# The first two tiles of a stage in one pass over the contraction, and an inverse root in nine dependent steps

## The chip, the cores and the metric

The kernel runs on one core of one Trainium2 chip. Its time is the device time of one execution in microseconds (us). A core has TensorE (PE, with its weight loads shown as PEld), VectorE (DVE), ScalarE (ACT), GpSimd (POOL) and SyncE (SP), which run their own instruction streams and meet at semaphores.

## The reference

A trunk of two layers over 256 tokens of width 1024, all in float32:

```python
for i in range(DEPTH):
    x = x + 0.5 * swiglu(rmsnorm(x, ln_ffn1[i]), w_ffn1_gu[i], w_ffn1_down[i])
    h = rmsnorm(x, ln_mix[i])
    x = x + (even_mixer(h, ...) if i % 2 == 0 else odd_mixer(h, ...))
    x = x + 0.5 * swiglu(rmsnorm(x, ln_ffn2[i]), w_ffn2_gu[i], w_ffn2_down[i])
    gate = jax.nn.sigmoid(rmsnorm(x, ln_ple[i]) @ w_ple_gate[i])
    x = x + gate * (p[i] @ w_ple_proj[i])
return rmsnorm(x, ln_final)

def rmsnorm(x, g):
    return x * lax.rsqrt(jnp.mean(x * x, axis=-1, keepdims=True) + EPS) * g
```

swiglu is (silu(h Wg) * (h Wu)) Wdown with an inner width of 2816. Each mixer is two kinds of eight-head attention between an input and an output projection.

## The kernel before

The residual stream lives transposed in SBUF as xT, [128 features, 8 blocks, 256 tokens]. To keep float32 accuracy in fast matmuls every operand is split into a high and a low part: ACT writes the high part of a weight chunk (L511) and DVE the low part (L746) into wsp, a ring of four chunks of two units each; SP loads the chunks into raw. For the stream, ACT writes the high part of a block (L571, xs_hi) and DVE the low part (L810, xs_lo) into xsA or xsB. A tile is 128 output features by 256 tokens, one PSUM bank; it goes over the KD = 8 blocks of the contraction in tile8. wide_product (L1072, L1073) does a block with two matmuls of 512 and 256 columns, product (L1063 to L1065) with three of 256. `ready` makes a block of the first tile wait for its xs_lo.

There are nine norms, 0 to 8. Norms 0, 2, 4, 6 open a gate/up stage (gate_up), 1 and 5 a mixer's input projection (mixer_in), 3 and 7 the gate of the per-layer embedding (ple, after eight small projection tiles "p"), and 8 the end. A stage starts its matmuls on the stream before it is normalised, and the norm is put in afterwards:

- ACT squares each new block (L574), POOL sums the squares (L465, L468, sq_added).
- column_sums (L1092) adds them over the partitions on PE, into bank 7, one column per 128 tokens. In gate_up and mixer_in it stands behind the first tile, in ple behind tile p4.
- inverse_root on DVE: var (L821), an inverse square root from a shifted bit pattern and three Newton turns (L822 to L831), and two diagonal matrices rdiag (L837). `step` gives each instruction a semaphore and waits for it. DVE then waits for row_done.
- spread_rows (L1102) on PE turns rdiag into a row of factors in bank 6: behind the third tile (gate_up tile (1, 0), mixer_in n = 2), and in ple behind gate tile g0. DVE copies it out as rstd (L839).

DVE does its instructions in the order of its own code, so nothing of it runs between the root's first step and rstd, weight splits included. Before PE writes a bank it waits for the bank's last reader (`reuse`, the dictionary `reader`). After `down` banks 0 and 1 hold its tiles 6 and 7, read by the residual additions (L869, L872). After `out` the banks turn by three: out_bank gives tiles 6 and 7 banks 0 and 1 in layer 0, and tile 6 bank 1, tile 7 bank 2 in layer 1 (their addition is L992). In ple the last tiles of the gate are processed by L1011, ACT's sigmoid (L708), L1018 and L1020.

In layer 1's mixer_in POOL computes three pieces of bias (L485) as soon as hankel has been loaded. At the end ACT and DVE scale the turned result by rcol (L733, L1045).

The names in the rows: ps is PSUM, wsp the split weights, sqsum the summed squares, osp the attention's output.

Of the kernel before, what the change touches and what calls it, by code (L numbers as in the profile page):

```python
# [5 lines left out]
ALU = mybir.AluOpType  # L6
# [7 lines left out]
P = 128  # L14
# [6 lines left out]
KD = D_MODEL // P  # L21
# [101 lines left out]
def trunk(nc, x, p, ln_ffn1, w_ffn1_gu, w_ffn1_down, ln_mix, w_in_even, b_forget, w_out_even, w_in_odd,  # L123
# [14 lines left out]
    with ExitStack() as ctx:  # L138
# [129 lines left out]
        def stream(norm):  # L268


            return xsB if norm == 4 else xsA
# [465 lines left out]
        def _(dve):  # L737
# [75 lines left out]
            def inverse_root(norm):  # L813


                def step(ins):
                    state["n"] += 1
                    ins.then_inc(nstep, 1)
                    dve.wait_ge(nstep, state["n"])
                dve.wait_ge(col_done, norm + 1)  # L820
                step(dve.tensor_scalar(var[:], ps[:, BANK_COL, 0:TOK], 1.0 / D_MODEL, EPS, ALU.mult, ALU.add))  # L821
                step(dve.tensor_scalar(rcol[:].bitcast(I32), var[:].bitcast(I32), 1, None, ALU.logical_shift_right))  # L822
                step(dve.tensor_scalar(rcol[:].bitcast(I32), rcol[:].bitcast(I32), -1.0, float(MAGIC), ALU.mult, ALU.add))
                step(dve.tensor_scalar(nhalf[:], var[:], -0.5, None, ALU.mult))
                for _ in range(2):
                    step(dve.tensor_tensor(rtmp[:], rcol[:], rcol[:], ALU.mult))
                    step(dve.tensor_tensor(rtmp[:], rtmp[:], nhalf[:], ALU.mult))
                    step(dve.scalar_tensor_tensor(rcol[:], rtmp[:], 1.5, rcol[:], ALU.add, ALU.mult))
                step(dve.tensor_tensor(rtmp[:], rcol[:], rcol[:], ALU.mult))
                step(dve.tensor_tensor(rtmp[:], rtmp[:], nhalf[:], ALU.mult))  # L830
                last = dve.scalar_tensor_tensor(rcol[:], rtmp[:], 1.5, rcol[:], ALU.add, ALU.mult)  # L831
                last.then_inc(rcol_ready, 1)
                dve.wait_ge(rcol_ready, norm + 1)
                if norm == 8:
                    return
                for t in range(TOK):
                    dve.tensor_scalar(rdiag[:, t], ident[:], rcol[:, t:t + 1], None, ALU.mult).then_inc(rdiag_ready, 1)  # L837
                dve.wait_ge(row_done, norm + 1)
                dve.tensor_scalar(rstd[:], ps[:, BANK_ROW, 0:SEQ], -1.0, None, ALU.mult).then_inc(rstd_ready, 1)  # L839
                dve.wait_ge(rstd_ready, norm + 1)  # L840
# [208 lines left out]
        def _(pe):  # L1049
# [3 lines left out]
            def reuse(bank):  # L1053
                if bank in reader:
                    pe.wait_ge(*reader[bank])
# [23 lines left out]
            def tile8(bank, slot, col, xs, xs_base=None, sem_=None, form=product):  # L1079
# [4 lines left out]
                mm.then_inc(tile_done, 1)  # L1084
                return mm

            def column_sums(norm):
                pe.wait_ge(sq_added, KD * (norm + 1))
                if norm in (2, 6):
                    pe.wait_ge(os_lo, KD * (1 + norm // 6))  # L1090
                for t in range(TOK):
                    mm = pe.matmul(ps[:, BANK_COL, t:t + 1], sqsum[:, t * P:(t + 1) * P], cumtri[:, 2 * P - 1:2 * P],  # L1092
                                   start=True, stop=True)
                mm.then_inc(col_done, 1)
# [10 lines left out]
            def chunk_ready(c, lap=0):  # L1105
                pe.wait_ge(lo, 2 * c + 2 + 2 * RING * lap)

            def gate_up(ph, norm):
                c0, F0 = ph.c0, ph.F0
                xs = stream(norm)  # L1110
                for r in range(2):
                    chunk_ready(c0 + r)
                    for n in range(2):
                        bank = 2 * r + n
                        reuse(bank)
                        tile8(bank, (c0 + r) % RING, n * P, xs, KD * norm if (r, n) == (0, 0) else None, xs_lo,
                              form=wide_product)
                        if (r, n) == (0, 0):
                            column_sums(norm)
                        if (r, n) == (1, 0):  # L1120
                            spread_rows(norm)
                pe.wait_ge(rstd_ready, norm + 1)
                if ph.which == 1:
                    pe.wait_ge(p_lo, ph.layer + 1)
                with pe.Fori(0, (ph.chunks - 2) // RING) as i:
                    for r in range(RING):
                        c, pair = c0 + 2 + r, 1 + r // 2
                        chunk_ready(c, lap=i)
                        for n in range(2):
                            if r % 2 == 0:  # L1130

                                pe.wait_ge(gu_sum, F0 + 2 * (pair - 2) + n + 1 + GU_START + RING * i)
                            tile8(gu_bank(2 * pair) + 2 * (r % 2) + n, c % RING, n * P, xs, form=wide_product)
                for b in range(4):
                    reader[b] = (gu_sum, F0 + KF - 1 + b % 2 + GU_START)
# [66 lines left out]
            def mixer_in(ph, norm):  # L1202
                xs = stream(norm)
                for n, (chunk, col, what, idx, scale) in enumerate(IN_TILES[ph.layer]):
                    bank, c = in_bank(n), ph.c0 + chunk
                    chunk_ready(c)
                    reuse(bank)
                    if what in "qk":
                        tile8(bank, c % RING, col, xs, KD * norm if n == 0 else None, xs_lo)
                    else:  # L1210
                        t, w = (idx[2], 256) if what == "v" else (idx, P)
                        view = wsp[:, c % RING, :, 0:KD * 256].rearrange("p s (k n) -> p s k n", k=KD)
                        token_tile(ps[:, bank, 0:w], t, xs, lambda k: view[:, :, k, col:col + w]).then_inc(tile_done, 1)
                    reader[bank] = written(ph.layer, n)
                    if n == 0:
                        column_sums(norm)
                    if n == 2:
                        spread_rows(norm)
                        if ph.layer == 0:
                            forget_logits(xs)  # L1220
                    if ph.layer == 0 and n == 3:
                        forget_sums()
                    if ph.layer == 0 and 4 <= n < 4 + HEADS:
                        forget_keys(n - 4)
                    for i in slots(ph.layer, n):
                        attention_step(ph.layer, i, norm)
# [122 lines left out]
            def ple(ph_proj, ph_gate, norm):  # L1349
                for kind, m in PLE_TILES:  # L1350
# [8 lines left out]
                            mm = product(bank, chunk_w(c % RING, k, m * P, D_MODEL), psp[:, k], k == 0, k == KPLE - 1)  # L1359
                        mm.then_inc(tile_done, 1)  # L1360
                    else:
                        tile8(bank, c % RING, (m % 2) * P, stream(norm), KD * norm if m == 0 else None, xs_lo)
                    reader[bank] = (proj_ready if kind == "p" else g_norm, KD * ph_proj.layer + m + 1)
                    if (kind, m) == ("p", 4):
                        column_sums(norm)
# [69 lines left out]
```

## Time and profile before

| | us |
|---|---|
| three runs | 1115.35, 1118.67, 1126.55; median 1118.67 |
| the profiled execution | 1115.28 |
| its span | 1113.6 |
| PE busy in it | 1080.0 |
| DVE, ACT, POOL busy | 773.6, 590.3, 82.8 |
| mean granted TensorE clock | 0.989 of full |

The span runs from the first to the last instruction; 1.7 us lie around it. The profile names who ended an idle time of an engine. A matmul's row shows its start and a modelled end, and neighbours overlap, so the work of a row of matmuls is best read from start to start.

### The profile page before, as it was taken

The numbers are of one execution on the slowest core, as the hardware profiler recorded it, in microseconds if no ns is written. First come the engines' busy times: TensorE is split into PE (matmuls) and PEld (weight loads), VectorE is DVE, ScalarE is ACT, GpSimd is POOL, SyncE is SP. The second block draws the span as 40 slices with busy tenths as digits, with TensorE's granted clock in tenths as the row PEclk, the third lists the DMA queues.
The fourth block names the chain that finished last, engine by engine and source line by source line (L and its number), as shares of the span: only waits on it lengthen the run. The fifth ranks groups of instructions, "written<-read, shape, count | busy, mean of one in ns | idle before, by whom it ended". The sixth has DMA issues, their size and how long they took to land.

```text
span 1113.6 us, 18550 instructions
## 1 busy us (share of the span) xinstructions
PE 1080.0 (97%) x6691; PEld 953.0 (86%) x6691; DVE 773.6 (69%) x1361; ACT 590.3 (53%) x1027; POOL 82.8 (7%) x112
## 2 busy tenths in 40 slices
PE   4999999999999999999999999998999999999996
PEld 3888888998888888888888888888987888888886
DVE  5887855666545887855689777667657698785566
ACT  5565545434445565545556565444555566554454
POOL 4000001000002000001020000014003200000102
PEclk9999999999999999999999999999999999999998
DMA  8656447563232756447546554566623275544731
GB/s 258 217 191 204 130 139 222 186 194 114 87 104 60 234 188 208 130 137 224 189 152 227 190 187 143 154 203 207 202 81 114 85 227 187 190 129 136 212 128 39
DMA packets 225848, 183.94 MB, mean 165 GB/s; under 512 B 4648, under 2 KB 224512, under 8 KB 225792
## 3 DMA queue, kind: packets, MB, share of 16 engines
q1 hardware_dynamic: 222688, 181.45, 52.0%
q10 hardware_dynamic: 3104, 1.77, 0.6%
q8 instruction: 32, 0.52, 0.2%
q14 instruction: 24, 0.20, 0.1%
HBM read 182.02 MB, written 1.06 MB: 164 GB/s over the span
## 4 chain that ended last, share of the span: by engine, by line
PE 89%; DVE 5%; issue 3%; ACT 2%; DMA 0%; SPq 0%; DVEq 0%; POOLq 0%; POOL 0%; ACTq 0%
PE ps L1072 43%; PE ps L1073 22%; PE ps L1063 5%; PE ps L1064 4%; PE ps L1065 4%; DVE wsp L746 2%; PE ps L1245 2%; PE ps L1294 2%; PE ps L1168 1%; PE ps L1169 1%; PE ps L1170 1%; ACT wsp L511 1%; PE ps L1263 1%; PE ps L1295 1%; DMA gin<-in_ln_final_dram 0%
## 5 line engine op out<-in xcount | busy, mean ns | idle before, releaser
L746 DVE TENSOR_TENSOR wsp<-raw,wsp 128x1024 fp32r<-128x1024 f32 (+1 forms) x382 | 423.3, 1124 | 69.1 <-ACT wsp L511 62.7
L1072 PE MATMUL ps<-xsA,wsp 128*128 128x512 f32 x1056 | 372.7, 397 | 4.5 <-DVE wsp L746 3.9
L511 ACT ACTIVATE wsp<-raw 128x1024 fp32r<-128x1024 f32 (+1 forms) x382 | 356.0, 958 | 32.4 <-PE ps L1065 30.1
L1073 PE MATMUL ps<-xsA,wsp 128*128 128x256 f32 x1056 | 296.8, 281 | 0.0
L1072 PE MATMUL ps<-hff,wsp 128*128 128x512 f32 x704 | 245.4, 394 | 0.0
L1072 PEld LDWEIGHTS ps<-xsA,wsp 128*128 128x128 f32 x1056 | 198.9, 188 | 52.2 <-issue 5.2
L1073 PEld LDWEIGHTS ps<-xsA,wsp 128*128 128x128 f32 x1056 | 200.7, 190 | 0.0
L1073 PE MATMUL ps<-hff,wsp 128*128 128x256 f32 x704 | 196.7, 279 | 0.0
L1072 PEld LDWEIGHTS ps<-hff,wsp 128*128 128x128 f32 x704 | 131.9, 187 | 30.4
L1073 PEld LDWEIGHTS ps<-hff,wsp 128*128 128x128 f32 x704 | 132.8, 189 | 0.0
L1072 PE MATMUL ps<-xsB,wsp 128*128 128x512 f32 x352 | 124.2, 398 | 2.3 <-DVE xsB L810 2.1
L761 DVE TENSOR_TENSOR sq<-ps,sq 128x512 f32<-128x512 f32 x88 | 60.5, 687 | 86.0 <-ACT sq L527 86.0
L1063 PE MATMUL ps<-xsA,wsp 128*128 128x256 f32 x360 | 106.8, 297 | 3.4 <-DVE wsp L746 3.4
L571 ACT ACTIVATE xsA<-xT,gains 128x256 fp32r<-128x256 f32 x56 | 28.4, 507 | 152.1 <-DVE xT L872 126.8
L527 ACT ACTIVATE sq<-ps 128x512 f32<-128x512 f32 x88 | 51.9, 589 | 106.4 <-PE ps L1073 106.4
L1064 PE MATMUL ps<-xsA,wsp 128*128 128x256 f32 x360 | 104.0, 289 | 0.0
L1065 PE MATMUL ps<-xsA,wsp 128*128 128x256 f32 x360 | 103.8, 288 | 0.0
L1073 PE MATMUL ps<-xsB,wsp 128*128 128x256 f32 x352 | 98.1, 279 | 0.0
L1072 PEld LDWEIGHTS ps<-xsB,wsp 128*128 128x128 f32 x352 | 66.7, 190 | 18.5 <-DVE xsB L810 2.6
L530 ACT ACTIVATE silu<-gate_n 128x256 f32<-128x256 f32 x88 | 36.8, 419 | 84.9 <-DVE gate_n L763 84.9
L1063 PEld LDWEIGHTS ps<-xsA,wsp 128*128 128x128 f32 x360 | 71.2, 198 | 5.8 <-DVE wsp L746 3.6
L1064 PEld LDWEIGHTS ps<-xsA,wsp 128*128 128x128 f32 x360 | 71.3, 198 | 0.1
(172 smaller groups left out, 1328.4 us busy)
## 6 DMA issues: line engine op xcount, KB each, us to landing
raw<-in_w_ffn_gu_dram SPq DMA_DIRECT2D x88, 1024.0 KB, 5.1
raw<-in_w_ffn_down_dram SPq DMA_DIRECT2D x64, 704.0 KB, 4.7
raw<-in_w_in_even_dram SPq DMA_DIRECT2D x12, 1024.0 KB, 5.4
raw<-in_w_in_odd_dram SPq DMA_DIRECT2D x9, 1024.0 KB, 5.3
raw<-in_w_ple_gate_dram SPq DMA_DIRECT2D x8, 1024.0 KB, 5.9
raw<-in_w_out_even_dram SPq DMA_DIRECT2D x4, 1024.0 KB, 5.2
raw<-in_w_out_odd_dram SPq DMA_DIRECT2D x4, 1024.0 KB, 5.2
raw<-in_w_ple_proj_dram SPq DMA_DIRECT2D x2, 1024.0 KB, 5.1
```

The source lines that it names most:

```text
L511: act.activation(wsp[:, s, 0, half * n:(half + 1) * n], raw[:, s, half * n:(half + 1) * n], ACT.Copy).then_inc(hi, 1)
L527: act.activation(cross[:], ps[:, b:b + 3:2, SEQ:], ACT.Copy).then_inc(gu_cross, 1)
L530: act.activation(silu[:], gate_n[:, 0], ACT.Silu).then_inc(gu_silu, 1)
L571: act.activation(stream(norm)[:, m, 0, :], xT[:, m], ACT.Copy, scale=gain(norm, m)).then_inc(xs_hi, 1)
L746: dve.tensor_tensor(wsp[:, s, 1, sl], raw[:, s, sl], wsp[:, s, 0, sl].bitcast(F32), ALU.subtract).then_inc(lo, 1)
L761: dve.tensor_tensor(cross[:], ps[:, b:b + 3:2, 0:SEQ], cross[:], ALU.add).then_inc(gu_sum, 1)
L1063: pe.matmul(out_, whi, moving[:, 0, :], start=first, stop=False)
L1064: pe.matmul(out_, whi, moving[:, 1, :], start=False, stop=False)
L1065: return pe.matmul(out_, wlo, moving[:, 0, :], start=False, stop=last)
L1072: pe.matmul(ps[:, bank, :], whi, moving.rearrange("p s t -> p (s t)"), start=first, stop=False)
L1073: return pe.matmul(ps[:, bank, SEQ:], wlo, moving[:, 0, :], start=False, stop=last)
L1245: mm = pe.matmul(S[:, sl], qT[rows, qt, t * P:(t + 1) * P], kT[rows, kt, 0:keys], start=True, stop=True)
```

## The change

It has two parts. The new first_tiles does the stage's first two tiles together: blocks 0 to 5 for both in turn, then blocks 6 and 7 of the first, then of the second. It takes the place of the two tile8 calls in gate_up, mixer_in and ple; column_sums now follows both tiles, spread_rows keeps its place behind the third tile (in ple it follows both). Both banks are waited for ahead of the first block. The second part rewrites inverse_root: nhalf and the shift go together, and each Newton turn is two steps of two [128, 1] instructions with operands by pointer, in place of three steps over [128, 2].

```diff
@@ inverse_root
                 step(dve.tensor_scalar(var[:], ps[:, BANK_COL, 0:TOK], 1.0 / D_MODEL, EPS, ALU.mult, ALU.add))
+                dve.tensor_scalar(nhalf[:], var[:], -0.5, None, ALU.mult).then_inc(nstep, 1)
+                state["n"] += 1
                 step(dve.tensor_scalar(rcol[:].bitcast(I32), var[:].bitcast(I32), 1, None, ALU.logical_shift_right))
                 step(dve.tensor_scalar(rcol[:].bitcast(I32), rcol[:].bitcast(I32), -1.0, float(MAGIC), ALU.mult, ALU.add))
-                step(dve.tensor_scalar(nhalf[:], var[:], -0.5, None, ALU.mult))
-                for _ in range(2):
-                    step(dve.tensor_tensor(rtmp[:], rcol[:], rcol[:], ALU.mult))
-                    step(dve.tensor_tensor(rtmp[:], rtmp[:], nhalf[:], ALU.mult))
-                    step(dve.scalar_tensor_tensor(rcol[:], rtmp[:], 1.5, rcol[:], ALU.add, ALU.mult))
...
+                def square_term(t):
+                    y = rcol[:, t:t + 1]
+                    return dve.tensor_scalar(rtmp[:, t:t + 1], y, y, nhalf[:, t:t + 1], ALU.mult, ALU.mult)
+
+                def corrected(t):
+                    y = rcol[:, t:t + 1]
+                    return dve.tensor_scalar(y, rtmp[:, t:t + 1], 1.5, y, ALU.add, ALU.mult)
+
+                for turn in range(3):
+                    square_term(0)
+                    step(square_term(1))
+                    corrected(0)
+                    last = corrected(1)
+                    if turn < 2:
+                        step(last)
@@ block.tensor
+            def first_tiles(banks, slot, xs, norm, form):
+                ks = [(n, k) for k in range(KD - 2) for n in range(2)]
+                ks += [(n, k) for n in range(2) for k in range(KD - 2, KD)]
+                for n, k in ks:
+                    ready = (xs_lo, KD * norm + k + 1) if n == 0 else None
+                    mm = form(banks[n], chunk_w(slot, k, n * P), xs[:, k], k == 0, k == KD - 1, ready)
+                    if k == KD - 1:
+                        mm.then_inc(tile_done, 1)
@@ gate_up
+                chunk_ready(c0)
+                for n in range(2):
+                    reuse(n)
+                first_tiles((0, 1), c0 % RING, xs, norm, wide_product)
+                column_sums(norm)
+                chunk_ready(c0 + 1)
+                for n in range(2):
+                    reuse(2 + n)
+                    tile8(2 + n, (c0 + 1) % RING, n * P, xs, form=wide_product)
+                    if n == 0:
+                        spread_rows(norm)
@@ mixer_in
-                    if what in "qk":
-                        tile8(bank, c % RING, col, xs, KD * norm if n == 0 else None, xs_lo)
+                    if n == 0:
+                        reuse(in_bank(1))
+                        first_tiles((bank, in_bank(1)), c % RING, xs, norm, product)
+                    elif what in "qk":
+                        if n > 1:
+                            tile8(bank, c % RING, col, xs)
@@ ple
-                        tile8(bank, c % RING, (m % 2) * P, stream(norm), KD * norm if m == 0 else None, xs_lo)
+                        if m == 0:
+                            reuse(ple_bank("g", 1))
+                            first_tiles((bank, ple_bank("g", 1)), c % RING, stream(norm), norm, product)
+                        elif m > 1:
+                            tile8(bank, c % RING, (m % 2) * P, stream(norm))
```

On PE, at the start of norm 2 of the kernel before, the last rows of the first tile, the column sums (L1092) and the second tile, with what each waits for (os_lo: the attention's output, sq_added: the summed squares, resid: a residual addition):

```order
1359 L1072 MATMUL ps<-xsA,wsp 128x512 [waits xs_lo]
1360 L1073 MATMUL ps<-xsA,wsp 128x256
1361 L1072 MATMUL ps<-xsA,wsp 128x512 [waits xs_lo]
1362 L1073 MATMUL ps<-xsA,wsp 128x256
1363 L1092 MATMUL ps<-cumtri,sqsum 128x1 [waits os_lo,sq_added]
1364 L1092 MATMUL ps<-cumtri,sqsum 128x1
1365 L1072 MATMUL ps<-xsA,wsp 128x512 [waits resid]
1366 L1073 MATMUL ps<-xsA,wsp 128x256
```

The same place on PE in the changed kernel, where wide_product is L1082 and L1083 and the column sums L1112:

```order
1371 L1082 MATMUL ps<-xsA,wsp 128x512 [waits xs_lo]
1372 L1083 MATMUL ps<-xsA,wsp 128x256
1373 L1082 MATMUL ps<-xsA,wsp 128x512 [waits xs_lo]
1374 L1083 MATMUL ps<-xsA,wsp 128x256
1375 L1082 MATMUL ps<-xsA,wsp 128x512
1376 L1083 MATMUL ps<-xsA,wsp 128x256
1377 L1082 MATMUL ps<-xsA,wsp 128x512
1378 L1083 MATMUL ps<-xsA,wsp 128x256
1379 L1112 MATMUL ps<-cumtri,sqsum 128x1 [waits os_lo,sq_added]
1380 L1112 MATMUL ps<-cumtri,sqsum 128x1
1381 L1082 MATMUL ps<-xsA,wsp 128x512 [waits resid,lo]
1382 L1083 MATMUL ps<-xsA,wsp 128x256
```

The column sums stand 16 instructions (a tile) later from the stage's first (number 1347 in both), and what follows them is the third tile. The wait for resid on bank 1 (number 1365 before) is now part of instruction 1347.

On DVE, the inverse root of norm 0 in the kernel before, from var to rstd:

```order
L821 TENSOR_SCALAR var<-ps 128x2
L822 TENSOR_SCALAR rcol<-var 128x2
L823 TENSOR_SCALAR rcol<-rcol 128x2
L824 TENSOR_SCALAR nhalf<-var 128x2
L826 TENSOR_TENSOR rtmp<-rcol 128x2
L827 TENSOR_TENSOR rtmp<-rtmp,nhalf 128x2
L828 SCALAR_TENSOR_TENSOR rcol<-rtmp,rcol 128x2
```

and in the changed kernel, from var to rstd:

```order
L821 TENSOR_SCALAR var<-ps 128x2
L822 TENSOR_SCALAR nhalf<-var 128x2
L824 TENSOR_SCALAR rcol<-var 128x2
L825 TENSOR_SCALAR rcol<-rcol 128x2
L829 TENSOR_SCALAR rtmp<-rcol,nhalf 128x1 x2
L833 TENSOR_SCALAR rcol<-rtmp,rcol 128x1 x2
```

Of three Newton turns the first stands here; each was three instructions and is now four, so the root has 16 instructions where it had 13.

## Rows read from the trace of the kernel before

**Rows 1.** The page, busy time, share of the span and instructions by engine.

```profile
PE 1080.0 (97%) x6691; PEld 953.0 (86%) x6691; DVE 773.6 (69%) x1361; ACT 590.3 (53%) x1027; POOL 82.8 (7%) x112
```

**Rows 2.** Waits of PE: engine, line, waited for; us in total, times, longest.

```profile
PE ps L1102 <- DVE rdiag L837: 2.7, 2, 1.3
```

**Rows 3.** Timeline, norm 1 start: start us, us, engine, line, operation, count [idle before].

```profile
205.56 0.28 PE L1063 MATMUL ps<-xsA,wsp 128*128 128x256 f32 x1
...
206.25 0.42 DVE L872 SCALAR_TENSOR_TENSOR xT<-ps,tile_s 128x256 f32<-128x256 f32 x1
...
208.43 0.57 PE L1092 MATMUL ps<-cumtri,sqsum 128*128 128x1 f32 x4
...
208.86 0.36 PE L1063 MATMUL ps<-xsA,wsp 128*128 128x256 f32 x1
```

**Rows 4.** Timeline, norm 2 start.

```profile
354.28 0.40 PE L1072 MATMUL ps<-xsA,wsp 128*128 128x512 f32 x1
...
355.81 0.42 DVE L992 TENSOR_TENSOR xT<-ps,xT 128x256 f32<-128x256 f32 x1
...
358.00 0.61 PE L1092 MATMUL ps<-cumtri,sqsum 128*128 128x1 f32 x4
```

**Rows 5.** Timeline, norm 6 start; the L992 row is tile 6's addition.

```profile
880.20 0.41 DVE L992 TENSOR_TENSOR xT<-ps,xT 128x256 f32<-128x256 f32 x1
...
881.23 0.40 PE L1072 MATMUL ps<-xsA,wsp 128*128 128x512 f32 x1
...
884.96 0.27 PE L1092 MATMUL ps<-cumtri,sqsum 128*128 128x1 f32 x1
```

**Rows 6.** Timeline of DVE: norm 3's root, its ends; the forget gate's pointer pairs.

```profile
547.41 0.15 DVE L821 TENSOR_SCALAR var<-ps 128x2 f32<-128x2 f32 x1
...
549.97 0.48 DVE L837 TENSOR_SCALAR rdiag<-ident,rcol 128x128 f32<-128x128 f32 x2
...
220.68 0.35 DVE L884 SCALAR_TENSOR_TENSOR fl<-ps,rcol,bf 128x8 f32<-128x8 f32 x2
221.06 0.36 DVE L888 SCALAR_TENSOR_TENSOR fl<-ps,rcol,fl 128x8 f32<-128x8 f32 x2
```

**Rows 7.** Timeline, norm 3: gate tile g0's first matmul, spread_rows, rstd.

```profile
545.93 0.28 PE L1063 MATMUL ps<-xsA,wsp 128*128 128x256 f32 x1
...
550.32 0.71 PE L1102 MATMUL ps<-rdiag,negones 128*128 128x128 f32 x4 [1.35 <-DVE rdiag L837]
...
551.06 0.42 DVE L839 TENSOR_SCALAR rstd<-ps 128x256 f32<-128x256 f32 x1 [0.61 <-PE ps L1102]
```

**Rows 8.** Timeline, norm 4; then a stretch: us, busy by engine, clock, DMA.

```profile
574.49 1.34 DVE L810 SCALAR_TENSOR_TENSOR xsB<-xT,gains,xsB 128x256 fp32r<-128x256 f32 x2
...
575.49 0.50 PE L1072 MATMUL ps<-xsB,wsp 128*128 128x512 f32 x1 [2.08 <-DVE xsB L810]
...
584.23 0.61 PE L1102 MATMUL ps<-rdiag,negones 128*128 128x128 f32 x4
...
576.80:580.00 3.20, 3.20 (x12) 2.81 (x13) 2.75 (x15) 2.41 (x3) 0.00 (x0) 0.50 0.36 97
```

**Rows 9.** Timeline, norm 5, layer 1's mixer; then a stretch as above.

```profile
769.41 8.44 POOL L485 TENSOR_TENSOR bias<-mask_chunk,hankel 128x1024 f32<-128x1024 f32 x3 [6.76 <-DMA hankel<-rel_scratch]
...
770.46 8.47 DVE L746 TENSOR_TENSOR wsp<-raw,wsp 128x1024 fp32r<-128x1024 f32 x3
...
774.69 3.16 POOL L485 TENSOR_TENSOR bias<-mask_chunk,hankel 128x1024 f32<-128x1024 f32 x1
...
775.86 0.58 PE L1063 MATMUL ps<-xsA,wsp 128*128 128x256 f32 x1 [3.37 <-DVE wsp L746]
...
774.70:781.40 6.70, 5.54 (x26) 5.54 (x27) 6.70 (x5) 0.01 (x1) 6.70 (x4) 0.50 0.49 157
```

**Rows 10.** Timeline, the last gate tile of norm 7, and the result's scaling.

```profile
1101.43 0.42 DVE L1011 TENSOR_TENSOR tile_s<-ps,rstd 128x256 f32<-128x256 f32 x1 [0.53 <-PE ps L1065]
...
1108.28 1.27 ACT L733 ACTIVATE yN<-ps,rcol 128x512 f32<-128x512 f32 x2 [3.67 <-DVE rcol L831]
```

More of the change, by code:

```diff
@@ L821, in inverse_root @@
                 step(dve.tensor_scalar(var[:], ps[:, BANK_COL, 0:TOK], 1.0 / D_MODEL, EPS, ALU.mult, ALU.add))
+                dve.tensor_scalar(nhalf[:], var[:], -0.5, None, ALU.mult).then_inc(nstep, 1)
+                state["n"] += 1
                 step(dve.tensor_scalar(rcol[:].bitcast(I32), var[:].bitcast(I32), 1, None, ALU.logical_shift_right))
                 step(dve.tensor_scalar(rcol[:].bitcast(I32), rcol[:].bitcast(I32), -1.0, float(MAGIC), ALU.mult, ALU.add))
-                step(dve.tensor_scalar(nhalf[:], var[:], -0.5, None, ALU.mult))
-                for _ in range(2):
-                    step(dve.tensor_tensor(rtmp[:], rcol[:], rcol[:], ALU.mult))
-                    step(dve.tensor_tensor(rtmp[:], rtmp[:], nhalf[:], ALU.mult))
-                    step(dve.scalar_tensor_tensor(rcol[:], rtmp[:], 1.5, rcol[:], ALU.add, ALU.mult))
-                step(dve.tensor_tensor(rtmp[:], rcol[:], rcol[:], ALU.mult))
-                step(dve.tensor_tensor(rtmp[:], rtmp[:], nhalf[:], ALU.mult))
-                last = dve.scalar_tensor_tensor(rcol[:], rtmp[:], 1.5, rcol[:], ALU.add, ALU.mult)
+                def square_term(t):
[11 more added lines that the diff above has]
+                        step(last)
                 last.then_inc(rcol_ready, 1)
@@ L1110, in gate_up @@
                 xs = stream(norm)
[L1111 to L1121, printed above, removed]
+                chunk_ready(c0)
[9 more added lines that the diff above has]
+                        spread_rows(norm)
                 pe.wait_ge(rstd_ready, norm + 1)
```

## The prediction

> **What bounds the kernel now.** Read the page's first part, then the waits of PE, then the timeline around each stage start, where the change works. PE is busy 97% of the span [rows 1], so time can only be won or lost where PE stands still, or runs at half its clock. There are nine such places: the starts for norm 0 to norm 7, and the end (norm 8). At each, PE needs three things that come late: the last residual block (its low half, xs_lo), the column sums' inverse root (as rdiag), and a free PSUM bank. The waits view gives 2.7 us in two waits for rdiag [rows 2]; the timeline shows them at norms 3 and 7. Another 2.08 us is waited for xsB at norm 4 [rows 8], and 3.37 us at norm 5 for a weight split [rows 9]. At norms 1 and 2 the old order waits little: 208.43 - 205.56 = 2.87 us for the eight blocks of norm 1's first tile, which is a tile without any wait [rows 3]; norm 2's takes 3.72 us, so 0.85 us is lost [rows 4]; norm 6's 3.73 us, 0.86 lost [rows 5]. That is all there is to win.
>
> **The bank wait (added).** first_tiles needs banks 0 and 1 before its first block. After `down` (norms 1 and 5) bank 1 holds tile 7, read by the last residual addition, which ends at 206.25 + 0.42 = 206.67; PE had begun at 205.56 [rows 3]. With 0.04 for the release PE begins 1.15 us later, and as nothing was lost in that tile before, nothing comes back: +1.15 at norm 1 and at norm 5. After layer 0's `out` (norm 2) bank 1 again holds tile 7: its addition ends at 355.81 + 0.42 = 356.23 against a start at 354.28, +2.00, of which the 0.85 no longer lost inside the tile comes off: +1.15 [rows 4]. Layer 1's `out` turns the banks differently: bank 1 holds tile 6, added by 880.20 + 0.41 = 880.61, before PE arrives at 881.23; there the change does what it says, -0.85 [rows 5]. Norms 0, 3, 4 and 7 have bank 1 free in time. What is queued behind this wait on PE is the whole stage; DVE and ACT wait for its tiles.
>
> **The inverse root (both edits).** Before, from the first step to rdiag: 549.97 - 547.41 = 2.56 us [rows 6], 13 steps of about 0.2. Now nine dependent steps, but 16 instructions, and the twelve [128,1] ones take operands by pointer. The nearest rows are the forget gate's pairs of pointer instructions: two, then the dependent two 0.38 us later (220.68 to 221.06) [rows 6]. Upper side: square_term has two pointers, which no row shows; with another 0.1 on each of its three pairs the root costs 3.3. Lower side: if the second of a pair costs 0.07 beyond a step of 0.2, as little as an instruction can, 2.3. I take the pair's row: three plain steps 0.6, nhalf beside them 0.1, six pairs of 0.38 are 2.3, sum 3.0: slower than before by 0.4.
>
> The Trainium skill (VectorE: DVE Perf Modes, section "Rules for kernel authors") says to lower the number of chained DVE instructions and not the semaphores between them. By that rule 16 for 13 would cost 16/13 of 2.56, 3.15 us; the trace agrees only in part, as its pairs overlap (0.35 us for two) [rows 6].
>
> Column sums now leave one tile, not two, before spread_rows. From the next tile's start (208.86, 0.43 after the sums' start [rows 3]) the sums end 0.14 later, DVE starts 0.04 later, the root takes 3.0, and PE was released 550.32 - 549.97 = 0.35 after rdiag began [rows 6, 7]: 3.53 us, against a tile of 2.87. A new wait of 0.66, and some 0.1 for restarting: +0.75 at each of norms 0, 1, 2, 5 and 6. At 2.3 us for the root there would be none; at 3.3, 1.05 each.
>
> **Norms 3 and 4.** In `ple` spread_rows comes after both gate tiles: it could follow 0.12 after 16 blocks, 545.93 + 5.75 = 551.69, not 550.32, and waits for nothing [rows 7]. PE wins 1.35 and the restart, 1.5. But DVE gets its row sum later: rstd started at 551.06, 0.75 after the row; now 551.69 + 0.65 = 552.34, +1.28. From there to norm 4's last xsB at 574.49 + 1.34 = 575.83 DVE is the busy one: two waits of 0.6 for a sigmoid, no other idle; the waits move with it. So xsB's block 7 comes at 577.1 and block 6 at 576.7, while PE, 1.5 us ahead (it began this stage at about 571.0, now 569.5), has 12 blocks of 0.36 and stands still from 573.8 to 576.7: 2.9 us in place of 2.08. Four blocks then remain to the sums, and then one tile in place of two: at full clock the row would come at about 582.2, 2.0 before the 584.23 of the old kernel. But the wait of 2.08 us was followed by 3.4 us at half the clock, 1.2 GHz in place of 2.4 (the 0.50 of [rows 8]), and a longer one will hardly be spared: 1.7 us of lost work, now with the sums in it. Together -0.3.
>
> **Norm 5.** With +1.15 and +0.75 DVE's first split there wants to start at 770.46 + 1.9 = 772.36. POOL's three bias instructions start at 769.41 whatever PE does (they wait for hankel) and a POOL and a DVE instruction take 3.16 us in turn; the first of POOL's ended near 771.6 (8.44 - 2 x 3.16 = 2.1 after its start) [rows 9]. DVE now comes during the second and waits for it until 773.7, then again for the third: its second split ends near 778.0, not 775.8. PE: +2.2 in all, the 1.9 included. Bounds: +1.1 (if half of it falls into the 6.7 us at half clock [rows 9], where lost time costs half) to +3.9 (one more such stretch of 3.4).
>
> That turns are whole instructions is the rule of the Trainium skill (SBUF — State Buffer, section "Who interferes with whom"): the shared port is held for a whole instruction. By sharing in proportion it would be +1.9; the row of 3.16 us each agrees with turns.
>
> **Norm 7 and the end.** PE wins 1.5 as at norm 3, but the last tile's DVE work started 0.53 us after the engine went idle [rows 10], so DVE's lateness of 1.3 eats most of it: with some 2.4 us a tile for DVE against 2.87 for PE, the last start is 1101.2, not 1101.43. -0.3. After the last column sums ACT waited 3.67 us for rcol [rows 10]: the root is bare there, +0.4.
>
> **The clock at norm 2.** A wait of 2.0 us is as long as norm 4's 2.08 that brought 3.4 us at 0.50; the 1.35 us of norm 3 brought none. I count one such stretch: +1.7 (bounds 0 and 3.4).
>
> **The sum.** Norm 0 +0.75; norm 1 +1.15 +0.75; norm 2 +1.15 +0.75 +1.7; norms 3 and 4 -0.3; norm 5 +2.2; norm 6 -0.85 +0.75; norm 7 -0.3; end +0.4: +8.15 us. All of it is on PE's path, as PE waits nowhere else to take it in. The profiled execution took 1115.28 us (span 1113.6), so 1123.4. The median of the three runs is 1118.67, their lowest 1115.35, close to the profiled one; as a median of the changed kernel may stand a little above its quiet execution, I say 1124.
>
> **Rivals.** (a) The root is short. The pairs cost 0.27: no wait before spread_rows, -0.3 at the end, norm 5's splits come at 771.6 on the edge of POOL's first turn. 8.15 - 3.0 - 0.7 - 1.0 = +3.4 to +1.7 without norm 2's clock: 1117 to 1119. For it: plain instructions of two elements take 0.16. Against: the pointer pairs. (b) The gains stand: also DVE catches up between norms 3 and 4, so the 2.08, its 1.7 of clock and 3.0 of rdiag go: about -5 us, 1110. For it: these waits are in the profile. Against: DVE's chain without idle [rows 7, 8]. (c) Slower than before by more than the measurement: the clock. If waits of 1.15 and of 2 to 3 us at norms 1, 2 and 4 each bring 6.7 us at 0.50, as at norm 5 [rows 9], 3.4 each in place of my 1.7 + 0 + 1.7: +6.8, 1130. The point that decides is whether the new waits of 1.15 and 2.0 us are followed by a clock of 0.50 (1.2 GHz in place of 2.4) as the 2.08 was; against: the 1.35 us at norm 3 were not. A root of 3.3 us goes to the same side (+0.3 x 6). (d) The change does not do what it says, since in three of eight starts the bank is what PE waits for: that is in my sum.
>
> **How the numbers follow.** Forecast 0.50; (a) 0.20; (b) 0.10; (c) 0.20. A measurement tells about 1% (11 us) from no change. Half of what lies under (c) and a little of the forecast is over 1% slower than 1118.67, with the doubt whether the base is 1115 or 1119: slower 0.18; faster 0.02 from (b); within 1% 0.80. Range: from (a)'s 1117 less the 1.7 that norms 3 and 4 win if the clock is spared there, 1115, to (c), 1131.
>
> **What would show it.** In the changed profile: waits for DVE xT (the additions) at norms 1, 2, 5 of about 1.15, 2.0 and 1.15; waits of some 0.66 for rdiag at six starts, none at norms 3 and 7; root 3.0 us from its first step to rdiag; xsB wait near 2.9 at norm 4; split wait at norm 5 of 3.4 to 4.3; clock at 0.50 near norm 2. Pair distances of 0.27 would prove (a) right, an xsB wait near zero (b), more than three half-clock stretches inside the span (c).

## The result, and the profile after

The changed kernel took 1124.71 us (median of 20 runs, 1118.97 to 1129.60), the kernel before 1119.63 (20 runs, 1113.09 to 1126.55). The ratio is 1.0043, 95% interval 1.0024 to 1.0062: 4.8 us slower, by 2.7 to 6.9, well inside 1%. The forecast was 1124. All ratios here compare fast executions alone, which leaves out only two of the twelve of e3.

The profiled executions took 1125.26 and 1115.28 us (spans of 1123.5 and 1113.6). Their distance of 10.0 us is not all the change's: 3.5 us of it belong to the execution (see e8 and e9), so that 6.5 us are to be explained. First the page of the changed kernel, its engine line, which answers to [rows 1]:

```profile
PE 1082.4 (96%) x6691; PEld 952.9 (85%) x6691; DVE 779.6 (69%) x1388; ACT 590.0 (53%) x1027; POOL 80.7 (7%) x112
```

PE has the same 6691 matmuls. DVE has 27 instructions more, three at each of the nine roots. The waits of PE in the changed kernel (waiting line, waited for: us in total, times, longest us), against [rows 2]; L1082 and L1083 are wide_product now, L1073 to L1075 product, L1122 spread_rows, L847 rdiag, L882 and L1002 the residual additions:

```profile
PE ps L1122 <- DVE rdiag L847: 6.4, 6, 1.7
PE ps L1082 <- DVE wsp L746: 4.2, 5, 3.5
PE ps L1112 <- POOL sqsum L468: 3.8, 1, 3.8
PE ps L1082 <- DVE xsB L810: 2.6, 2, 1.7
PE ps L1073 <- DVE xT L882: 2.4, 2, 1.2
PE ps L1082 <- DVE xT L1002: 2.0, 1, 2.0
```

Three changes are there at a glance: the wait for rdiag went from 2.7 us in two waits to 6.4 in six, and 4.4 us are waited for residual additions where none was. The wait of 3.37 us for a weight split at norm 5 [rows 9] is gone. The timeline shows the additions' waits at the starts of norm 1 and norm 2, where [rows 3, 4] had none:

```profile
207.93 0.36 PE L1073 MATMUL ps<-xsA,wsp 128*128 128x256 f32 x1 [1.20 <-DVE xT L882]
...
359.80 0.47 PE L1082 MATMUL ps<-xsA,wsp 128*128 128x512 f32 x1 [2.05 <-DVE xT L1002]
```

The root of norm 1 on DVE, to be laid beside [rows 6], and below it what PE waits for it at norms 0, 1, 2 and 6:

```profile
214.30 0.16 DVE L821 TENSOR_SCALAR var<-ps 128x2 f32<-128x2 f32 x1 [5.56 <-PE ps L1112]
...
214.97 0.45 DVE L829 TENSOR_SCALAR rtmp<-rcol,nhalf 128x1 f32<-128x1 f32 x2
215.46 0.34 DVE L833 TENSOR_SCALAR rcol<-rtmp,rcol 128x1 f32<-128x1 f32 x2
215.83 0.46 DVE L829 TENSOR_SCALAR rtmp<-rcol,nhalf 128x1 f32<-128x1 f32 x2
...
217.55 0.48 DVE L847 TENSOR_SCALAR rdiag<-ident,rcol 128x128 f32<-128x128 f32 x2
```

```profile
30.82 0.38 PE L1122 MATMUL ps<-rdiag,negones 128*128 128x128 f32 x1 [0.74 <-DVE rdiag L847]
...
217.89 0.38 PE L1122 MATMUL ps<-rdiag,negones 128*128 128x128 f32 x1 [0.66 <-DVE rdiag L847]
...
369.65 0.35 PE L1122 MATMUL ps<-rdiag,negones 128*128 128x128 f32 x1 [0.83 <-DVE rdiag L847]
...
900.85 0.35 PE L1122 MATMUL ps<-rdiag,negones 128*128 128x128 f32 x1 [0.84 <-DVE rdiag L847]
```

From var to rdiag are 217.55 - 214.30 = 3.25 us, where it was 2.56. A pair with two pointers takes 215.46 - 214.97 = 0.49 us to the next step, a pair with one 215.83 - 215.46 = 0.37.

Norms 3 and 4, which answer to [rows 7, 8]: rstd of norm 3, the two waits of PE for the stream at norm 4, its last two low blocks, and the stretch behind (us, busy by engine, clock, DMA):

```profile
557.96 0.42 DVE L849 TENSOR_SCALAR rstd<-ps 128x256 f32<-128x256 f32 x1 [1.21 <-PE ps L1122]
...
579.72 0.50 PE L1082 MATMUL ps<-xsB,wsp 128*128 128x512 f32 x1 [0.89 <-DVE xsB L810]
...
581.41 1.34 DVE L810 SCALAR_TENSOR_TENSOR xsB<-xT,gains,xsB 128x256 fp32r<-128x256 f32 x2
...
582.42 0.50 PE L1082 MATMUL ps<-xsB,wsp 128*128 128x512 f32 x1 [1.73 <-DVE xsB L810]
```

```profile
583.50:586.70 3.20, 3.20 (x13) 2.81 (x13) 2.15 (x9) 2.64 (x3) 0.00 (x0) 0.50 0.23 60
```

Here 581.41 + 1.34 = 582.75 is the end of norm 4's last low block. From rstd's start to that end it is 582.75 - 557.96 = 24.79 us, before 575.83 - 551.06 = 24.77: DVE's chain moved as a whole. Norm 5, against [rows 9]. The first row is the root's first step in the kernel before, the others are of the changed kernel:

```profile
763.35 0.16 DVE L821 TENSOR_SCALAR var<-ps 128x2 f32<-128x2 f32 x1 [1.30 <-PE ps L1092]
```

```profile
777.98 6.45 POOL L485 TENSOR_TENSOR bias<-mask_chunk,hankel 128x1024 f32<-128x1024 f32 x3 [7.24 <-DMA hankel<-rel_scratch]
...
778.96 3.42 DVE L847 TENSOR_SCALAR rdiag<-ident,rcol 128x128 f32<-128x128 f32 x2
...
780.30 0.38 PE L1122 MATMUL ps<-rdiag,negones 128*128 128x128 f32 x1 [1.68 <-DVE rdiag L847]
...
782.43 0.58 PE L1122 MATMUL ps<-rdiag,negones 128*128 128x128 f32 x1 [1.64 <-DVE rdiag L847]
```

The two rdiag instructions, 0.48 us elsewhere, took 3.42 beside POOL's bias: each ended with one of POOL's. The end, against [rows 10]:

```profile
1114.37 0.27 PE L1112 MATMUL ps<-cumtri,sqsum 128*128 128x1 f32 x1 [3.79 <-POOL sqsum L468]
...
1118.27 1.26 ACT L733 ACTIVATE yN<-ps,rcol 128x512 f32<-128x512 f32 x2 [4.36 <-DVE rcol L833]
```

PE leaves norm 7 1.5 us ahead, but the sum of the squares (L468) is done only 0.56 us earlier against the stage, so PE waits 1.0 us longer for them (3.79 in place of 2.80); rcol takes 4.36 - 3.67 = 0.69 us more.

How much later PE runs, stage by stage, next to the forecast's terms. Each number is the growth, across a stage's start, of the distance between the same matmul in the two profiles:

| place | forecast, us | measured, us |
|---|---|---|
| norm 0 | +0.75 | +1.06 |
| norm 1 | +1.90 | +2.31 |
| norm 2 | +1.90, and +1.7 for the clock | +2.30 |
| norms 3 and 4 | -0.3 | -0.75 |
| norm 5 | +2.2 | +1.6 |
| norm 6 | -0.10 | +0.12 |
| norm 7 and end | +0.1 | +0.12 |
| sum | +8.15 | +6.8 |

0.2 us of norm 4's are already in the 3.5 us of the execution (a longer distance from block to block, see e8), and small shifts inside the stages take 0.1: that is the 6.5.

### The profile page after: what moved, and what is told of

Its sections match the earlier page's. It is cut to its first block, busy times and chain, and to the rows that moved or that the text cites. A ratio compares the mean times of both kernels' runs of the same rounds, so it can differ in the third digit from the quotient of the medians.

```text
span 1123.5 us, 18584 instructions
## 1 busy us (share of the span) xinstructions
PE 1082.4 (96%) x6691; PEld 952.9 (85%) x6691; DVE 779.6 (69%) x1388; ACT 590.0 (53%) x1027; POOL 80.7 (7%) x112
## 3 DMA queue, kind: packets, MB, share of 16 engines
HBM read 182.02 MB, written 1.06 MB: 163 GB/s over the span
## 4 chain that ended last, share of the span: by engine, by line
PE 88%; DVE 7%; issue 3%; ACT 1%; DMA 0%; SPq 0%; DVEq 0%; POOLq 0%; POOL 0%; ACTq 0%
PE ps L1082 42%; PE ps L1083 21%; PE ps L1073 5%; PE ps L1074 4%; PE ps L1075 4%; DVE wsp L746 2%; PE ps L1269 2%; PE ps L1318 2%; PE ps L1188 1%; PE ps L1189 1%; PE ps L1190 1%; PE ps L1287 1%; DVE rtmp L829 1%; DVE silu L1028 1%; PE ps L1319 1%
## 5 line engine op out<-in xcount | busy, mean ns | idle before, releaser
L746 DVE TENSOR_TENSOR wsp<-raw,wsp 128x1024 fp32r<-128x1024 f32 (+1 forms) x382 | 418.8, 1113 | 69.5 <-ACT wsp L511 62.8
L1082 PE MATMUL ps<-xsA,wsp 128*128 128x512 f32 x1056 | 372.1, 397 | 6.1 <-DVE wsp L746 4.1
L1083 PE MATMUL ps<-xsA,wsp 128*128 128x256 f32 x1056 | 295.9, 280 | 0.0
L1082 PE MATMUL ps<-hff,wsp 128*128 128x512 f32 x704 | 246.6, 395 | 0.0
L1082 PEld LDWEIGHTS ps<-xsA,wsp 128*128 128x128 f32 x1056 | 199.1, 189 | 53.6 <-issue 5.2
L1083 PEld LDWEIGHTS ps<-xsA,wsp 128*128 128x128 f32 x1056 | 200.2, 190 | 0.0
L1083 PE MATMUL ps<-hff,wsp 128*128 128x256 f32 x704 | 196.9, 280 | 0.0
L1082 PEld LDWEIGHTS ps<-hff,wsp 128*128 128x128 f32 x704 | 132.1, 188 | 31.4
L1083 PEld LDWEIGHTS ps<-hff,wsp 128*128 128x128 f32 x704 | 132.8, 189 | 0.0
L1082 PE MATMUL ps<-xsB,wsp 128*128 128x512 f32 x352 | 126.3, 403 | 2.8 <-DVE xsB L810 2.6
L1073 PE MATMUL ps<-xsA,wsp 128*128 128x256 f32 x360 | 106.8, 297 | 2.4 <-DVE xT L882 2.4
L1075 PE MATMUL ps<-xsA,wsp 128*128 128x256 f32 x360 | 103.8, 288 | 0.0
L1083 PE MATMUL ps<-xsB,wsp 128*128 128x256 f32 x352 | 99.4, 282 | 0.0
L1082 PEld LDWEIGHTS ps<-xsB,wsp 128*128 128x128 f32 x352 | 66.7, 190 | 20.2 <-DVE xsB L810 3.3
L1073 PEld LDWEIGHTS ps<-xsA,wsp 128*128 128x128 f32 x360 | 71.2, 198 | 5.1 <-issue 5.0
```

The costliest lines, as they stand in the source:

```text
L746: dve.tensor_tensor(wsp[:, s, 1, sl], raw[:, s, sl], wsp[:, s, 0, sl].bitcast(F32), ALU.subtract).then_inc(lo, 1)
L1073: pe.matmul(out_, whi, moving[:, 0, :], start=first, stop=False)
L1075: return pe.matmul(out_, wlo, moving[:, 0, :], start=False, stop=last)
L1082: pe.matmul(ps[:, bank, :], whi, moving.rearrange("p s t -> p (s t)"), start=first, stop=False)
L1083: return pe.matmul(ps[:, bank, SEQ:], wlo, moving[:, 0, :], start=False, stop=last)
```

## The experiments

Device times are medians; the kernel before ran beside them, with a median of 1119.06 us for e1 to e4 and 1117.58 for e5 to e7. Since single executions of one kernel lie up to 14 us apart (1108.98 to 1122.99 in the second batch of before), single causes are read from the waits of the profiles and the totals from the medians.

**e1: the order of tiles alone.** The old root in the changed kernel.

```diff
-                for turn in range(3):
-                    square_term(0)
-                    step(square_term(1))
-                    corrected(0)
-                    last = corrected(1)
+                for _ in range(2):
+                    step(dve.tensor_tensor(rtmp[:], rcol[:], rcol[:], ALU.mult))
...
```

> The changed order of tiles with the old root of 13 steps. Theory 1 (the new root is what makes PE wait for rdiag): the waits for rdiag at norms 0, 1, 2 and 6, 0.66 to 0.84 us in the changed kernel, shrink by the 0.69 us that the root is shorter (3.25 to 2.56), to 0.2 or less; the bare root at the end is 0.7 shorter. Of the 6.9 us by which the changed kernel's stages are late some 3.5 go: +3.4 us against before. Rival (the moved column sums, not the root, make the wait): the waits stay at 0.6 or more and the kernel stays near +6. The waits for bank 1 (1.2, 2.05, 1.2 us) stay as they are in both.

Measured: 1123.30 us against 1119.06 of before, ratio 1.0030 (1.0001 to 1.0058). The root stands at 2.56 us again, and one wait for rdiag over 0.15 us is left, at norm 2; the additions' waits are unchanged:

```profile
370.30 0.35 PE L1112 MATMUL ps<-rdiag,negones 128*128 128x128 f32 x1 [0.15 <-DVE rdiag L837]
```

```profile
PE ps L1063 <- DVE xT L872: 2.4, 2, 1.2
PE ps L1072 <- DVE xT L992: 2.0, 1, 2.0
```

So with the sums moved it is the root's length that decides: 0.69 us less of it, and the waits at norms 0, 1, 2 and 6 are all but gone. It takes both parts, as e2 shows: the long root in the old order makes no wait at these starts. At norm 5 the shorter root was over before POOL's bias began, and PE waited 3.1 us for a split there instead. The ratio gives +3.4 us, the number expected; its interval (0.1 to 6.5) would bear others too, so the waits decide.

**e2: the root alone.** The old order with the new inverse_root.

> The old order of tiles with the new root. Theory 1: the root takes 3.25 us where it took 2.56, and it is bare at three places: norms 3 and 7 (PE waits for rdiag 2.0 instead of 1.35 us) and the end. Together +2.1 us; nothing at the other starts, where two tiles hide it. Rival (fewer dependent steps are quicker on the whole, and only the crowded place of the changed kernel is slow): root 2.3 us, waits 1.1 us, -0.8 us.

Measured: 1123.01 us, ratio 1.0031 (1.0007 to 1.0055), +3.5 us for the expected +2.1, which the interval holds (0.8 to 6.2). Waits of PE:

```profile
PE ps L1112 <- DVE rdiag L847: 4.0, 2, 2.0
```

Where [rows 2] had 2.7 us in two waits there are 4.0 in two. The nine steps are slower than the thirteen wherever they stand bare. The rival falls.

The longer wait did one thing more, which the expectation had not counted. Behind the one at norm 3 TensorE's clock fell for 3.4 us, which it did behind none of the waits of 1.2 to 1.35 us there in the other profiles; behind the 1.97 us at norm 7 it did not:

```profile
549.34 0.58 PE L1112 MATMUL ps<-rdiag,negones 128*128 128x128 f32 x1 [2.02 <-DVE rdiag L847]
```

```profile
549.50:552.70 3.20, 3.20 (x15) 3.20 (x16) 1.98 (x3) 0.00 (x0) 0.00 (x0) 0.50 0.24 83
```

**e3: bank 1 waited for later.** In the changed kernel:

```diff
-                ks = [(n, k) for k in range(KD - 2) for n in range(2)]
+                ks = [(n, k) for n in range(2) for k in range(KD - 2)]
                 ks += [(n, k) for n in range(2) for k in range(KD - 2, KD)]
                 for n, k in ks:
+                    if (n, k) == (1, 0):
+                        reuse(banks[1])
```

and the early waits for the second bank left out. Blocks 0 to 5 of the two tiles no longer alternate either: the later wait needs that, and the run doesn't tell the two apart.

> The changed kernel, but first_tiles does blocks 0 to 5 of the first tile, then 0 to 5 of the second, and waits for bank 1 only there. Theory 1 (the early wait for bank 1 is pure loss): the waits of 1.2, 2.05 and 1.2 us for the residual additions at norms 1, 2 and 5 go, and no other wait grows by more than 0.3, so -4.4 us against the changed kernel, +2.5 against before. Rival (the wait only moves): the stream's block 7, or the squares' sum, is then what PE waits for at the same starts, 1 us or more, and less than 2 us are won. At norm 5 the root may finish before POOL's bias begins; then the wait for rdiag goes there and the one of 3.4 us for the weight split comes back.

Measured: 1121.05 us, 2.0 above the median of before, ratio 0.9999 (0.9967 to 1.0030). The interval, -3.7 to +3.4 us, holds the expected +2.5 and no loss at all, so here too the waits decide. No wait for a residual addition is left at norms 1, 2 and 5; these stay:

```profile
PE ps L1124 <- DVE rdiag L847: 4.5, 6, 0.8
...
PE ps L1073 <- DVE wsp L746: 2.9, 1, 2.9
PE ps L1082 <- DVE xsB L810: 2.4, 1, 2.4
```

The wait did not move to the stream or the squares (2.4 us for xsB and 3.8 for the squares, 2.6 and 3.8 in the changed kernel). At norm 5 the root now ends before POOL begins: 0.67 us for rdiag, and the split's wait is back with 2.9, as the expectation had it for that case.

**e4: the embedding's gate as before.** e1 with ple's tiles in the old order (spread_rows after g0).

> The changed order in the gate/up and mixer stages only; the per-layer embedding's gate and the root as before. Against the run with the order alone (e1). Theory 1 (in the embedding stage DVE is the bound, and rstd one tile later makes the stream of norm 4 late): the waits for rdiag of 1.35 us at norms 3 and 7 are back, the stream's last low block at norm 4 is 1.3 us earlier against the stage's start, the wait for xsB falls from 2.6 to under 1 us and the clock doesn't fall there: 1.3 to 3 us less than e1. Rival (the wait saved on PE is saved for good): 2.7 us more than e1.

Measured: 1120.74 us, ratio 1.0000 (0.9974 to 1.0025), 2.6 us below e1 by the medians, which alone would be within the noise of both; but the rival's +6 over before lies outside the interval. The waits of 1.3 us for rdiag at norms 3 and 7 are back. There is no wait for xsB at all, and no half clock at norm 4: from norm 3 to norm 4 this kernel is 2.6 us ahead of e1 in the profile. So DVE sets the pace there, and in the changed kernel the wait saved at norm 3 was paid back at norm 4. The profile showed something else besides, at norm 5 (DVE's old root, POOL's bias, PE):

```profile
775.42 2.04 DVE L830 TENSOR_TENSOR rtmp<-rtmp,nhalf 128x2 f32<-128x2 f32 x1
777.50 2.10 DVE L831 SCALAR_TENSOR_TENSOR rcol<-rtmp,rcol 128x2 f32<-128x2 f32 x1
779.63 2.63 DVE L837 TENSOR_SCALAR rdiag<-ident,rcol 128x128 f32<-128x128 f32 x2
```

```profile
775.26 6.45 POOL L485 TENSOR_TENSOR bias<-mask_chunk,hankel 128x1024 f32<-128x1024 f32 x3 [6.97 <-DMA hankel<-rel_scratch]
```

```profile
781.85 0.58 PE L1112 MATMUL ps<-rdiag,negones 128*128 128x128 f32 x1 [5.67 <-DVE rdiag L837]
```

Instructions of two elements, 0.16 us elsewhere, took 2.04 and 2.10, because POOL's came first. The wait for rdiag was 5.67 us.

e1 has the same order and the same root at norm 5 and had no such wait, because POOL began later in it: 775.94 against the root's first step at 772.78, 3.2 us behind it, in e4 775.26 against 773.25, 2.0 us. In the two profiles of the changed kernel it was 2.3 and 2.6 us. What norm 5 loses is thus in part a matter of the execution.

**e5: both parts mended.** Gate/up and mixer stages only, blocks ordered as in e3, the column sums moved forward, the root in the old form with nhalf beside the shift:

```diff
                     if k == KD - 1:
                         mm.then_inc(tile_done, 1)
+                        if n == 0:
+                            column_sums(norm)
@@ inverse_root
+                dve.tensor_scalar(nhalf[:], var[:], -0.5, None, ALU.mult).then_inc(nstep, 1)
...
-                step(dve.tensor_scalar(nhalf[:], var[:], -0.5, None, ALU.mult))
```

> The order of tiles mended: gate/up and mixer stages only, bank 1 waited for at the second tile's first block, column sums between the first tile's end and blocks 6 and 7 of the second; the root is the old one with nhalf beside the shift (12 dependent steps, 2.43 us). Theory: no wait for a residual addition, none for rdiag at norms 0, 1, 2, 4, 6 (two blocks and a tile, 3.6 us, cover 3.0), 0.85 us won at norms 2 and 6, 2.1 at norm 4 and no fall of the clock there, 0.1 at norms 3, 7 and the end; at norm 5 POOL's bias decides: between 0 and 4 us lost if it meets the root's instructions with two inputs in SBUF, as in e4 (5.7 us waited). -6 to -2 us against before, so at least as quick as both. Rival (the overlap of two tiles is worth nothing, since something else comes late at these starts): waits of 0.5 us or more for anything else at norms 2, 4 and 6, and no time below before.

Measured: 1111.30 us against 1117.58, ratio 0.9944 (0.9915 to 0.9973), 6.3 us faster than before, just past the expected -6 to -2. Waits of PE:

```profile
PE ps L1063 <- DVE wsp L746: 3.8, 1, 3.8
...
PE ps L1116 <- DVE rdiag L837: 2.4, 2, 1.2
```

The two waits for rdiag are those of norms 3 and 7, each 0.1 to 0.2 shorter; at norms 2, 4 and 6 nothing over 0.25 us is waited for. Overlapping the first two tiles does pay where no new wait comes with it; the rival falls. How the gain divides among the four edits was not measured. Norm 5 keeps its wait for a split.

**e6: POOL's bias held back as well.** In e5:

```diff
             pool.wait_ge(pv_done, 2 * HEADS)
+            pool.wait_ge(*written(1, 2))
```

> As e5, but POOL begins its bias of layer 1 only when the mixer's third tile has been read. Theory 1 (at norm 5 POOL's whole instructions hold up DVE): no wait above 0.5 us at norm 5, no fall of the clock behind it: 3.4 us of waiting and some 2 to 3 of clock less than before there, -8 to -10 us against before in all. Rival (the bias is needed in time): attention's first step waits for it and PE stands still later, as long.

Measured: 1106.13 us (seven executions, 1103.88 to 1109.12) against 1117.58, ratio 0.9906 (0.9872 to 0.9941): 11.5 us faster than before by the medians, 10.5 by the ratio, and 5.2 below e5. Waits of PE, and the stretch behind norm 5's first tiles:

```profile
PE ps L1117 <- DVE rdiag L838: 2.4, 2, 1.2
...
PE ps L1064 <- DVE wsp L747: 0.4, 1, 0.4
```

```profile
764.00:785.00 21.00, 20.62 (x173) 20.42 (x172) 19.36 (x30) 10.51 (x11) 9.72 (x4) 1.00 0.66 213
```

The clock is 1.00 through the stage, the wait 0.4 us, and PE waits for nothing else over 0.2 us until norm 6, so the later bias holds up nothing. This version beats both kernels.

**e7: the hold alone on the changed kernel.**

> The changed kernel with the same hold on POOL's bias. Theory 1: of the 1.7 + 1.6 us that PE waits for the two halves of rdiag at norm 5 only the 0.66 of the other starts is left, and the clock doesn't fall behind it (6.8 us at half): 4 to 6 us less than the changed kernel. Rival (the wait is the root's own length): it stays above 2 us.

Measured: 1120.92 us against 1117.58, ratio 1.0049 (1.0022 to 1.0076). The waits for rdiag fell from 6.4 us to 4.3, none over 0.84, though a sixth at norm 4 (0.53) came in:

```profile
PE ps L1123 <- DVE rdiag L848: 4.3, 6, 0.8
```

```profile
360.30:363.50 3.20, 3.20 (x12) 2.71 (x11) 1.83 (x2) 3.20 (x5) 0.60 (x1) 0.50 0.02 6
```

By the tiles' ends norm 5 is 4.8 us better than in the changed kernel, as expected, and the clock does not fall there. But it fell at norm 2 (the last row, 1.7 us), and the medians show none of the gain: the ratio to before is that of the changed kernel. Among the profiles a gain is there: with the longer distances taken off as under e9, e7's span is 1119.4 - 7.0 = 1112.4 us, against 1116.5 and 1116.6 of the two profiles of the changed kernel. The cause of the wait is shown, its worth for the median is not.

**e8: the kernel before, once more.**

> The kernel before, unchanged, for a second profile. If the two distances from block to block (0.347 and 0.353 us), between which the stages of all profiles so far change, are a matter of the execution and not of the kernel, then the stages that have the longer one fall otherwise here than in the first profile (there only the last gate/up stage), the distance changes only across a stretch at half the clock, and the stages' starts agree within 0.1 us. If it is the kernel's, it is again the last stage alone.

**e9: the changed kernel, once more.**

> The changed kernel, unchanged, for a second profile. Theory (the clock's fall after the wait of 2.0 us at norm 2 is a matter of the execution: it came in e1, e4 and e7, which have that wait, and not in the first profile of the changed kernel): the waits are the same to 0.1 us (1.2, 2.05, 1.2 for the additions, 6.4 in six for rdiag), while the stretches at half the clock and the stages with the longer distance from block to block may fall otherwise; a fall at norm 2 is likelier than not. Rival (they belong to the kernel): the same stretches and the same stages as in the first profile.

Measured: spans of 1114.1 (device time 1115.82) and 1116.6 us (1118.35), against 1113.6 and 1123.5 of the first profiles. What differs is seen in stretches of 40 us inside gate/up stages, all at clock 1.00. In the first profile of before, norm 6:

```profile
920.00:960.00 40.00, 40.00 (x228) 34.63 (x228) 30.22 (x42) 22.11 (x35) 0.00 (x0) 1.00 0.58 189
```

in the first profile of the changed kernel, norm 4:

```profile
600.00:640.00 40.00, 40.00 (x228) 34.64 (x227) 33.27 (x46) 25.18 (x40) 0.00 (x0) 1.00 0.64 211
```

in e8, norms 2 and 4:

```profile
380.00:420.00 40.00, 40.00 (x229) 34.72 (x228) 32.60 (x46) 24.02 (x37) 0.00 (x0) 1.00 0.61 203
600.00:640.00 40.00, 40.00 (x233) 35.29 (x232) 34.03 (x48) 25.88 (x40) 0.00 (x0) 1.00 0.63 208
```

and in e9, norm 4:

```profile
600.00:640.00 40.00, 40.00 (x233) 35.28 (x232) 34.03 (x49) 25.68 (x40) 0.00 (x0) 1.00 0.65 214
```

PE does 232 or 228 matmuls in the same time. Averaged, the distance from one block's L1072 (L1082) to the next is 0.3467 or 0.3533 us, nothing between, and it holds for a whole gate/up and down stage: 528 blocks, 3.5 us. The first profile of before has the long distance in one such stage (norm 6), e8 in one (norm 2), the first of the changed kernel in two (norms 4 and 6), e9 in none. Taken off, before is 1110.1 and 1110.6, the changed kernel 1116.5 and 1116.6: in these profiles the change costs 5.9 to 6.5 us. The stretches at half the clock still differ among them: 17.1 us in each of three, 13.6 in e9. Two parts of e8's expectation fell. The distance changes not only across a stretch at half the clock: in e5 and e6 it changed between norms 2 and 4 with no such stretch there. And the stages' starts do not all agree within 0.1 us: against the first profile of before, e8's norm 0 was 0.5 shorter, norm 5 0.4 shorter, and norm 4, with 6.8 us at half the clock in place of 3.4, 1.4 longer. What sets the distance stays open.

e9's waits are those of the first profile but for rdiag, 7.2 us in seven (0.52 at norm 4, 1.94 + 1.64 at norm 5). Its clock fell at norm 2, and not at norm 4. Together: with the wait of 2.0 us at norm 2 the clock fell behind it in four profiles of five (e1, e4, e7, e9, not the first of the changed kernel), without it in none of six (before, e2, e3, e5, e6, e8). At norm 4, behind waits of 1.8 to 2.6 us for xsB, it fell in six of eight.

## Why the prediction was right

**The bank wait** was right to 0.05 us: 1.20, 2.05 and 1.2 for 1.15, 2.00 and 1.15, and none at norm 6. e3 showed that the place of the wait makes it, and that nothing else is late there.

**The inverse root** was right in kind, 0.25 us too short in size: the term "six pairs of 0.38" was mis-sized. Pairs with one pointer take 0.37, the row's 0.38; those with two take 0.49, the upper side that the text had named. Three more pairs of 0.12 are 0.36; with nhalf and the plain steps a little cheaper it came to 3.25. PE waited 0.66 to 0.84 us, and lost 1.06 at norm 0 where 0.75 was forecast. e1 and e2 tell the root from the order. The estimate by the number of instructions, 16/13 of 2.56, gave 3.15, nearer than the sum, though the pairs do overlap.

**Norms 3 and 4**: the step on which it rested, DVE's chain carried over whole, held to 0.02 us, and e4 showed it from the other side. PE waited 0.89 + 1.73 = 2.62 us, forecast 2.9, and the clock fell for 3.4 us. The stage starts cost -0.75 in place of -0.3.

**Norm 5** was near only in its sum, +1.6 for +2.2, and that is luck. The step "DVE's first split there wants to start at 772.36" failed: DVE did not get to its splits. The root was over only after POOL's bias had begun (778.96 against 777.98), so that rdiag itself, not a split, waited for POOL's instructions, and when the splits' turn came POOL was on its last. The prediction's own terms, with one more row of the same trace, say so: the root's first step stood at 763.35 before, a tile and the bank wait later is 763.35 + 2.87 + 1.15 = 767.37, and a root of 3.0 us from there ends at 770.4, behind POOL's start at 769.41. It moved DVE's work behind the root by 1.9 us, and left out that the root itself starts a tile later. e7 confirms POOL as the cause, e4 shows how much worse it can be.

**Norm 7 and the end** were right in sum, +0.12 for +0.1, because two errors cancel: DVE's work came out 0.56 us earlier (forecast 0.3), and the bare root cost 0.69 (forecast 0.4).

**The clock at norm 2** did not fall in the profile to be explained, so this term of 1.7 is missing in its 6.5 us; in four of the five profiles with that wait it did.

Of the rivals, (a), a short root, is refuted by the pair distances, (b) by the wait for xsB (and its -5 us does not follow from the terms that it names: 8.15 less 2.08, 1.7 and 3.0 is +1.4), (c) by the stretches at half the clock: three inside the span (norms 1, 4, 5), as before. In (d) the measured bank waits make half of the loss: 1.2 + 1.2 at norms 1 and 2, and 1.2 at norm 5, of 6.5 us. The sum of 8.15 was 1.7 too high against its own profile. That is as much as the clock's term, but only since the others' errors cancel: the starts of norms 0, 1, 2 and 6 cost some 1.3 us more than forecast without it, norms 3, 4 and 5 together 1.05 less, and 0.2 are counted in the execution's 3.5. That the median met 1124 to 0.7 us is luck: the base there, 1119.63, is 4.4 above the profiled execution's 1115.28, and the step from it was 5.1 us by the medians where 8.15 was summed.

## What to carry to other kernels

When work is moved so that PE can begin on two tiles together, wait for each buffer at its own first use, and count the shortest cover that is left for every small chain on another engine. Fewer dependent steps are no gain by themselves: time the pair of instructions that takes a step's place, with its operands. And where a stage's start hangs on DVE, keep long POOL instructions that read SBUF out of it; on this kernel that was worth 5.2 us on top of the mended order (e6), though nothing that the median of the changed kernel shows (e7).

## What the hardware showed unexpectedly

- In the changed kernel's trace a DVE instruction on one column with two operands by pointer has its successor's start 0.19 us later and its dependent's at 0.30; with one pointer 0.13 and 0.25. The plain ones on two columns, in the trace of before, took 0.20 to the dependent one.
- POOL's 2.15 us instructions (e4, norm 5) held up DVE instructions of 0.16 us (TENSOR_TENSOR and SCALAR_TENSOR_TENSOR with two inputs in SBUF) for their whole length, and rdiag (TENSOR_SCALAR, 128x128), but not, in the changed kernel, the one-column TENSOR_SCALAR with pointers that began 0.1 us after POOL's (778.09, 0.27 us as elsewhere). The Trainium skill (SBUF — State Buffer, section "Who interferes with whom") has a rule that fits: a DVE instruction with two SBUF inputs contends with a POOL instruction that reads SBUF, one in a two-port mode contends with POOL too, and others do not. Whether rdiag ran in such a mode no run here shows.
- TensorE's blocks of 768 columns came at 0.3467 or at 0.3533 us, at a granted clock of 1.00, constant through a stage and different from one execution of the same kernel to the next. Four such stages make up to 14 us; with stretches at half the clock that last 3.4 us in one execution and 6.8 in another (norm 5: 6.8 in the first profile of before, 3.4 in e8) they would be enough for the 10 to 14 us between executions of one kernel; that they are the whole of it was not shown.
